# Last block of a two-block transformer kernel: the groups' shares turned as 24 rows and spread over the features by transfers through DRAM

## What is computed

```
for g, (offs, bias, kg_all, vg_all) in enumerate(cfg):
    ...
    lse = jax.nn.logsumexp(s, axis=-1)
    p = jnp.exp(s - lse[..., None])
    outs.append(jnp.einsum('bhqk,bqkhd->bqhd', p, vg.astype(jnp.float32)))
    lses.append(lse)
wts = jax.nn.softmax(jnp.stack(lses, axis=0), axis=0)
out = jnp.sum(wts[..., None] * outs, axis=0)          # one weight per token, head and group
...
y_a = (_multiscale_pool(a_in, ...) * jax.nn.silu(a_gate)) @ w_proj_a
y_b = (att * jax.nn.silu(b_gp)) @ w_proj_b
merged = gates[:, :, 0] * y_a + gates[:, :, 1] * y_b
x = x + merged @ w_out
```

## Time and profile before

| | |
|---|---|
| median of 3 runs | 1302.85 us (1302.75, 1302.85, 1304.57) |
| the profiled execution's own time | 1302.51 us |
| its span in the trace | 1300.7 us |
| busy share: PE, DVE, ACT, POOL | 99%, 71%, 52%, 10% |
| mean granted TensorE clock | 0.999 |

### The profile page before, as it was taken

One profiled execution on the slowest core, in us unless ns is written; L12 is line 12 of the kernel. 1 busy time (PEld: TensorE's weight loads), 2 busy tenths in 40 slices (PEclk: granted clock), 3 DMA queues, 4 the chain that ended last, 5 costly groups with the idle time before them and its releaser, 6 DMA issues.

```text
span 1300.7 us, 16758 instructions
## 1 busy us (share of the span) xinstructions
PE 1283.2 (99%) x6242; PEld 1057.4 (81%) x6242; DVE 929.7 (71%) x1298; ACT 679.3 (52%) x976; POOL 125.9 (10%) x190
## 2 busy tenths in 40 slices
PE   9999999999999999999999999999999999999997
PEld 6888888888888888888887777888888887788886
DVE  6878948986678956677875677667895656655674
ACT  7444537755444546544445567644444735566542
POOL 1000003711000000000001230000000133200000
PEclk9999999999999999999999999999999999999999
DMA  9665645228565655666564643466564496445541
GB/s 311 216 201 189 210 140 203 66 82 263 191 194 194 202 186 162 195 194 194 194 196 158 231 162 119 149 194 194 194 226 154 170 293 215 156 137 179 174 149 33
DMA packets 149505, 236.29 MB, mean 182 GB/s; under 512 B 10080, under 2 KB 104464, under 8 KB 148928
## 3 DMA queue, kind: packets, MB, share of 16 engines
q1 hardware_dynamic: 144432, 222.26, 52.6%
q0 software_dynamic: 4640, 12.81, 3.3%
q10 hardware_dynamic: 368, 0.37, 0.1%
HBM read 233.27 MB, written 4.47 MB: 183 GB/s over the span
## 4 chain that ended last, share of the span: by engine, by line
PE 91%; DVE 4%; ACT 3%; issue 1%; POOL 0%; DMA 0%; POOLq 0%; SPq 0%; ACTq 0%; DVEq 0%
PE acc L628 20%; PE acc L630 20%; PE acc L629 20%; PE acc L661 7%; PE acc L662 7%; PE acc L665 7%; PE misc L704 4%; DVE wl L2086 1%; ACT wh L1538 1%; PE misc L1339 1%; PE misc L888 1%; PE misc L1195 1%; ACT xh L1584 0%; PE acc L868 0%; ACT hn L1570 0%
## 5 line engine op out<-in xcount | busy, mean ns | idle before, releaser
L2086 DVE TENSOR_TENSOR wl<-raw,wh 128x2048 fp32r<-128x2048 f32 x199 | 450.6, 2270 | 183.5 <-ACT wh L1538 182.8
L1538 ACT ACTIVATE wh<-raw 128x2048 fp32r<-128x2048 f32 x205 | 383.5, 1894 | 125.3 <-PE acc L665 104.2
L628 PE MATMUL acc<-wh,xh 128*128 128x512 f32 (+1 forms) x832 | 324.5, 390 | 3.3 <-DVE xl L2132 1.6
L630 PE MATMUL acc<-wh,xl 128*128 128x512 f32 (+1 forms) x832 | 322.5, 388 | 0.0
L629 PE MATMUL acc<-wl,xh 128*128 128x512 f32 (+1 forms) x832 | 322.3, 387 | 0.0
L628 PEld LDWEIGHTS acc<-wh,xh 128*128 128x128 f32 x832 | 156.2, 188 | 36.7 <-DVE wl L2074 1.8
L630 PEld LDWEIGHTS acc<-wh,xl 128*128 128x128 f32 x832 | 156.2, 188 | 32.2
L629 PEld LDWEIGHTS acc<-wl,xh 128*128 128x128 f32 x832 | 156.2, 188 | 31.1
L1633 ACT ACTIVATE sg<-acc,rstd 128x256 f32<-128x256 f32 x88 | 41.4, 475 | 240.4 <-PE acc L630 240.3
L2252 DVE STREAM_TRANSPOSE aT<-a_n 32x384 f32<-32x384 f32 (+1 forms) x256 | 137.1, 536 | 3.9
L661 PE MATMUL acc<-wh,ah 128*128 128x512 f32 x320 | 124.8, 390 | 0.0
(11 more groups left out here) (365 smaller groups left out, 1613.1 us busy)
## 6 DMA issues: line engine op xcount, KB each, us to landing
raw<-in_ffn_w_in_dram SPq DMA_DIRECT2D x170, 512.0 KB, 4.8
raw<-in_ffn_w_out_dram SPq DMA_DIRECT2D x88, 512.0 KB, 4.3
raw<-in_w_in_dram SPq DMA_DIRECT2D x64, 512.0 KB, 4.7
raw<-in_fox_w_in_dram SPq DMA_DIRECT2D x24, 512.0 KB, 4.2
raw<-in_ple_w_gate_dram SPq DMA_DIRECT2D x16, 512.0 KB, 4.4
raw<-in_mla_w_o_dram SPq DMA_DIRECT2D x8, 512.0 KB, 4.0
raw<-in_fox_w_o_dram SPq DMA_DIRECT2D x8, 512.0 KB, 4.4
raw<-in_w_out_dram SPq DMA_DIRECT2D x8, 512.0 KB, 4.4
```

The costliest lines, as they stand in the source:

```text
L628: pe.matmul(dst, hi, rhs_h, start=first, stop=False)
L630: return pe.matmul(dst, lo, rhs_h, start=False, stop=last)
L1538: act.activation(wh[:, s, 0:n], raw[:, s, 0:n], ACT.Copy).then_inc(hi_done, 1)
L2086: dve.tensor_tensor(wl[:, s, 0:n], raw[:, s, 0:n], wh[:, s, 0:n].bitcast(F32), ALU.subtract)\
```

## The change

The shares are no longer spread over features before they are turned. PE turns the 24 columns of `cmb` themselves, once for each 128 tokens (two transposes of 24 rows), directly after the pooling branch's transposes after c = 12. DVE copies the 24 x 256 result out of `misc` into `srow` at the end of c = 12, behind its work on `yal`. POOL writes `srow` to DRAM, waits for that, and reads it back with six transfers, each of which repeats four heads' rows over 64 partitions (1 KB pieces, 256 KB a transfer), two for each group's tile `wide[j]`. DVE's `share(j)` multiplies from there, in whole tiles of 128 x 1024. `share(2)` now stands at w = 29, ahead of the reading of chunk 14. ACT's three spreading instructions and 24 of PE's transposes are gone. In POOL's order the new transfers stand between `bg` and `fg`.

```diff
-SHARE_FILLS = (2, 2, 1, 1)
+SHARE_FILLS = (1, 0, 0, 0)
...
-        wide = [mg[:, 0, :].rearrange("p (t n) -> p t n", t=NT), mg[:, 1, :].rearrange("p (t n) -> p t n", t=NT),
-                otmp[:, :, :]]
+        wide = [v.rearrange("p (k n) -> p k n", k=4)
+                for v in (mg[:, 0, :], mg[:, 1, :], otmp.rearrange("p t n -> p (t n)"))]
...
+        srow = qT2[0:G3 * H8, 0:S]
...
+        shares_d = nc.dram_tensor("shares_by_token", (G3 * H8, S), F32, kind="Internal")
...
-        share_wide = sem("share_wide")
+        shares_out = sem("shares_out")
+        share_in = [sem(f"share_in{n}") for n in range(G3)]
...
-            def turn_shares(j):
-
-
-                pe.wait_ge(share_wide, j + 1)
-                for b in (2 * (j % 2), 2 * (j % 2) + 1):
-                    open_m(b, hr[b] + U_FILLS[b] + j // 2)
-                    for k in range(2):
-                        for t in range(NT):
-                            o, c = k * S + t * P, (2 * (b % 2) + k) * P
-                            mm = turn(b, slice(o, o + P), wide[j][:, t, c:c + P])
-                    mm.then_inc(m_ready[b], 1)
+            def turn_shares():
+
+                pe.wait_ge(shares, 1)
+                open_m(0, hr[0] + U_FILLS[0])
+                for t in range(NT):
+                    w = G3 * H8
+                    mm = turn(0, slice(t * P, (t + 1) * P), cmb[:, 1, t * w:(t + 1) * w], w)
+                mm.then_inc(m_ready[0], 1)
...
                     turn_fill(q + B2_YAT, s_a)
-                if c == 13:
-                    turn_shares(0)
-                    turn_shares(1)
+                    turn_shares()
                 if c == 14:
-                    turn_shares(2)
...
-                    if w == B2_COMBINE + 1:
-                        act.wait_ge(shares, 1)
-                        part = cmb[:, 1, :].rearrange("p (t g h) -> p t g h", t=NT, g=G3)
-                        for n in range(G3):
-                            act.activation(wide[n].rearrange("p t (h d) -> p t h d", d=HD),
-                                           part[:, :, n, :].unsqueeze(3).to_broadcast([P, NT, H8, HD]), ACT.Copy)\
-                               .then_inc(share_wide, 1)
...
             def share(j):
 
 
-                for b in range(2):
-                    m = 2 * (j % 2) + b
-                    dve.wait_ge(m_ready[m], hf[m] + U_FILLS[m] + j // 2 + 1)
-                    o, to = oraw[:, j, 2 * b:2 * b + 2, :], yt[:, 2 * b:2 * b + 2, :]
-                    e = dve.tensor_tensor(o if j else to, pair(M[:, m, :]), o, ALU.mult)
-                    if j:
-                        link(e)
-                        p = 2 * (1 - j % 2) + b
-                        dve.wait_ge(m_read[p], hr[p] + U_FILLS[p] + 1)
-                        e = dve.tensor_tensor(to, to, o, ALU.add)
-                    e.then_inc(m_read[m], 1)
+                dve.wait_ge(share_in[j], 16 * 2)
+                o = oraw[:, j, :, :]
+                link(dve.tensor_tensor(o if j else yt, wide[j], o, ALU.mult))
+                if j:
+                    link(dve.tensor_tensor(yt, yt, o, ALU.add))
...
-                    dve.wait_ge(m_read[b], B2_END[b])
...
                         share(1)
+                    if w == B2_COMBINE + 5:
+                        share(2)
                     if w == B2_COMBINE + 6:
-                        share(2)
                         gate_outputs()
...
+                    dve.wait_ge(m_ready[0], hf[0] + U_FILLS[0] + 1)
+                    dve.tensor_copy(srow, M[0:G3 * H8, 0, 0:S]).then_inc(m_read[0], 1)
...
+            pool.wait_ge(m_read[0], B2_END[0])
+            pool.dma_start(shares_d[:, :], srow).then_inc(shares_out, 16)
+            pool.wait_ge(shares_out, 16)
+            for j in range(G3):
+                for lane in range(2):
+                    pool.dma_start(wide[j][HD * lane:HD * lane + HD, :, :],
+                                   bass.AP(shares_d, (H8 * j + lane) * S, [[0, HD], [2 * S, 4], [1, S]]))\
+                        .then_inc(share_in[j], 16)
             pool.wait_ge(m_ready[2], HEADS["b2"][0][2] + 2 * NU)
             pool.dma_start(fg[:, :], bass.AP(I["final_gain_2"].tensor, 0, [[0, P], [1, D]])).then_inc(fg_in, 16)
```

## The result

The changed kernel is **slower**, by a little that is clear of the noise: 1306.9 us median against 1302.88 (22 executions each), ratio 1.0026 with a 95% interval of 1.0019 to 1.0033. The medians differ by 4.0 us, the means of the same executions by 3.45 us, which is the 1.0026. I had forecast no change that can be told (1303.8, range 1301.2 to 1306.2). The profiled execution took 1305.91 us with a span of 1304.0, against 1302.51 and 1300.7: 3.3 us are in the trace.

The account below looks back on a forecast made before the run. From chunk 14's reading to PA's second group, DVE and ACT were taken to set the time, PE less than 1 us from being the bound. +0.90 and 0.05 us on the 1302.85 median gave 1303.8 us, range 1301.2 to 1306.2.

Parts of the forecast that it names:

- PE's part: After chunks 13 and 14, 2.50 us of turns removed; two turns added after c = 12, taken at 0.05 us.
- ACT's part: Three spreadings of 1.04 us removed in 1204.7 to 1207.7; nothing gained, since ACT waits for DVE afterwards.
- DVE's part: Copy at 1214.16 hidden; five share operations at 1.25 us with handover, 6.25 us in all; work barely shrinks.
- The move of share(2): Ahead of chunk 14's reading, it makes PE begin chunk 15 at 1236.89 instead of 1235.59, 1.30 us later.
- What comes back: At PA's seventh matmul the 0.40 us stall for g + 33 goes, leaving PE +0.90 us.
- The transfers: DRAM reads for DVE's shares, 8.0 us each, land in time: first pair by 1225, last by 1227.5.
- rival 2: Transfers come late, DVE waits in share(0); with 15.7 us landings 5.3 us more, 1309.1; chance 0.08.
- The clock: PE's 3.8 us idle before chunk 15 counted without a clock loss, being shorter than the 4.9 us seen at full level.
- rival 3: PE's 3.8 us idle stretch before chunk 15 costs its clock: 1.5 us, 1305.3, or 1306.8 at twice the length; chance 0.12.
- my +0.95: Whole kernel's forecast shift: +0.90 us at PA's seventh matmul, carried to the end, plus 0.05 us of c = 12.

Follow-up runs that it names:

- the run with PE kept busy: Changed kernel with 36 idle transposes on PE in the gap before chunk 15; ratio 1.0009 to the kernel before, stretch 75.93 us.
- the run with the earlier turn: Changed kernel with only the two turns and srow's copy moved ahead, so transfers start 3 us earlier; ratio 1.0019 to the kernel before, stretch 77.09 us.
- `share(2)` as before: Changed kernel with share(2) at the head of w = 30, where the kernel before has it; ratio 1.0009 to that kernel, stretch 74.54 us.
- the kernel before reordered: Kernel before with only share(2) moved directly behind the reading of chunk 14; ratio 0.9993 to the kernel before, stretch 74.17 us.
- the rearranged one: Changed kernel with turns and copy earlier, share(0) behind chunk 13's reading, share(2) behind chunk 14's; ratios 0.9983 and 0.9988 to the kernel before.

## Why the prediction was wrong

By its own steps:

- **PE's part.** Turns removed 2.50 us: held. PE was through at 1233.25, worked out 1233.1. The two turns after c = 12 cost nothing that can be seen (chunk 13 begins 1.49 us after the start of chunk 12's reading, before and after).
- **ACT's part.** Held; nobody noticed that its three operations were gone.
- **DVE's part.** The `share` operation was worked out at 1.22 us and 1.25 with its handover; it is 1.22 to 1.23, and 1.26. An estimate by the Trainium skill's formula for a float32 `tensor_tensor` addition, (N + 151) / 0.96 ns (VectorE: DVE Perf Modes, the TRN2 errata section), is 1.224 us for 1024 elements; the trace agrees. The copy took 0.40 us and was hidden.
- **The move of share(2).** Held, and it is the root: the reading of chunk 14 ends at 1236.9 without a late transfer (1236.84 worked out; 1237.44 less 0.57 measured), and PE begins chunk 15 1.9 us later than before, 1.3 without the late transfer (1.30 worked out), with 2.5 us less to do.
- **What comes back.** Held: no wait for g + 33.
- **The transfers: mis-sized.** I took every read at 8.0 us from issue to landing and the second pair to have landed 1.5 us before its use (by the prediction's own times it is 1.9); the last of that pair took 10.9 us and was 0.57 us late (0.15 and 1.27 in other executions). The median of another stage's row did not fit this one: the reads ran beside 2 MB of weights from 1216.5 on. Issued 3 us earlier the same reads took 4.3 us and not 7.8, those for the third tile 6.1 and not 13.0. It cost 0.6 us, and I had put it at nothing. I had this as rival 2, with too high a price and too small a chance.
- **The clock: the step that failed.** I put the idle stretch at no cost beyond its length and gave rival 3, the clock lost in it, a chance of 0.12, on the ground that in the earlier trace rows the clock had held for 4.9 us of idleness. One such event bounds nothing: the clock fell 4.0 us into one stretch and not at all in the 3.70 us of another, but just behind it. In all four profiles with an idle stretch of 3.7 us or more (4.24, 3.82, 3.70, 3.70) the clock fell, once in it and three times as it ended or up to 1 us behind it; in those with 2.42 and 1.6 us it held. The price I named, 1.5 us, was right: 1.45 in the profile, 1.4 by the run with PE kept busy, up to 1.6 in the others. The row it came from was the right one, though it is no row of the granted clock: the windows of those first 5 us show the full level, but the weight loads of the nine matmuls stand 0.43 us apart, the pitch of the slow matmuls here. The Trainium skill (TensorE: Matmul & The Clock Gate, "HAM oscillation") tells of waits between bursts of matmuls after which the next burst starts at the half rate, and I had used the page only for a rival. The traces agree in part: a slow stretch came with each of the four waits, but two of the four bursts started at full rate, and falls came with shorter waits elsewhere (last section).
- **A term I had not.** From DVE's last operation to the end of the span it is 5.66 us after, 5.14 before. The closing wait of SP for PE is the difference (waits of SP in the last 6 us, after, then before):

```profile
SPq L155 <- PEq L155: 0.9, 1, 0.9
```

```profile
SPq L155 <- PEq L155: 0.4, 1, 0.4
```

  It is 0.9 or 1.0 in all eight profiles with the transfers, and 0.4 in the four without, the run that leaves out only them among these. That it goes with the transfers is shown; why the close of the program takes longer with them is open.

With my +0.95 plus 0.6 for the late landing, 1.45 for the clock and 0.5 at the close, less 0.2 of small change, one is at the 3.3 us of the profile, and near the 3.45 by which the means differ. Late landing and close alone, without the clock, would have given 1304.9 us, inside my range; with the clock it is 1306.3, just outside. The long executions are those with the lower mean clock: 0.997 for the profiled 1305.91 us, 0.994 for 1309.40 and 0.993 for 1311.33. That is what falls of the clock at other places would give; no long execution of this kernel was profiled.

## What to carry to other kernels

When an engine that is busy 99% of the time is relieved, ask first which other engine must act before it may go on; here that was one reading of an accumulator, and a 2.5 us operation put ahead of it turned a saving of 2.5 us into a loss. Put such work behind the reading, where the engine waits anyway. And price an idle stretch of TensorE like this one, 3.7 us or more, at its length plus the slow matmuls that come with it (1.4 to 1.6 us here in each of four profiles), not at its length. The waits of 2.42 and 1.63 us cost nothing more here, but no run shows a length that is safe.

## What the runs showed of the hardware that I had not expected

The clock can fall after PE has taken up work again: about 0.5 us later in the run with the earlier turn and 1.0 us later in the second profile of the changed kernel, each time for some eight matmuls at 0.43 us. In all four profiles the clock stayed at the half level for 3.4 us.

And it falls elsewhere, with shorter waits. Three of the executions profiled (without transfers, `share(2)` as before, the kernel before reordered) show the half level twice ahead of the last block, for 3.4 us each time. The clock falls at 7.6 to 8.7 us, 0.5 to 0.8 us behind a wait of PE of 1.86 to 2.31 us, and again at 256.8 to 257.9 us, 0.1 to 0.4 us behind a wait of 1.09 us. In the other nine the wait at the first place was 0.98 to 1.59 us, at the second the same 1.09, and no window at either place shows a fall. The windows of the one without transfers:

```profile
10.00:15.00 5.00, 5.00 (x24) 4.11 (x23) 2.98 (x8) 3.14 (x9) 0.76 (x2) 0.84 1.10 353
...
255.00:260.00 5.00, 3.91 (x19) 3.09 (x18) 4.77 (x16) 3.29 (x11) 2.29 (x3) 0.73 0.00 0
```

Those three reach chunk 13's reading at 1223.9 to 1225.0 instead of 1220.7 to 1221.2. A fourth, with PE kept busy, reaches it at 1222.8: its matmuls stand 0.43 us apart until 10.3 us, although the windows give the full clock there. Near the start of an execution the pitch of the matmuls tells more than the column of the clock.

So executions whose programs are the same up to there differ by up to 4 us before the changed place is reached, more than the change is worth. Only a stretch measured inside the trace, between two events around the change, separates the versions: it repeated within 0.01 us for the kernel before, 0.02 us for the rearranged one, and 0.23 us for the changed one, whose wait for the transfers was 0.57 us and then 0.15.
